# Two attention layers on one Trainium2 core: the first differential pair weighs its values one step of the lanes later

## What is computed

```python
z = rmsnorm(h) @ w_in[l]
c_q, c_kv, k_rope, dq, dk, dv, p_in, z_gate = split(z)
# latent attention (MLA), 8 heads of 64 + 32
q = (rmsnorm(c_q) @ w_uq);  kv = rmsnorm(c_kv) @ w_ukv
p = softmax(causal(scale * (q_nope k_nope + rope(q_rope) rope(k_rope))))
y_mla = p @ v
# differential attention, 8 heads with two maps each
p = softmax(causal(scale * dq dk - slope * distance))      # maps 0 and 1
y_diff = rmsnorm((p[0] - lam * p[1]) @ dv) * (1 - lambda_init)
y_pool = pool_mixer(p_in)
branches = [y_mla, y_diff, y_pool] @ w_branch;  gates = sigmoid(z_gate)
h = h + sum(gates * branches) @ w_out
```

## Time and profile before

| | |
|---|---|
| median of 3 runs | 2029.14 us (2028.71 to 2029.24) |
| the profiled execution | 2028.63 us, of which the span from first to last instruction is 2026.8 us |
| PE busy | 2015.5 us, 99% of the span |
| PEld, DVE, ACT busy | 84%, 69%, 50% |
| DMA engines busy | 54% by the hardware queue |
| granted clock of TensorE | 0.999 of full speed |
| mixer of layer 0 with its first visits, 236 to 380 us | PE 142.2, DVE 116.8, ACT 99.5 us of 144 |

### The profile page before, as it was taken

The page is one execution under the profiler, slowest core; times in us unless marked ns, Lnnn a source line. Parts: engine busy times, 40 slices in busy tenths (PEclk is TensorE's granted clock), DMA queues, the critical chain, the costliest instruction groups (busy, mean ns, idle before and its releaser), DMA issues.

```text
span 2026.8 us, 24812 instructions
## 1 busy us (share of the span) xinstructions
PE 2015.5 (99%) x10220; PEld 1701.7 (84%) x10220; DVE 1391.4 (69%) x1657; ACT 1022.1 (50%) x1218; POOL 88.5 (4%) x128
## 2 busy tenths in 40 slices
PE   9999999999999999999999999999999999999998
PEld 7888878888888888878888888888888888888887
DVE  6655697775757676787675667657767577577675
ACT  6444568453445345667453356654534466545331
POOL 1001010000010001100100000000100000000000
PEclk9999999999999999999999999999999999999999
DMA  9655544465656555444566574654655555555552
GB/s 335 212 187 169 174 164 146 162 207 195 193 182 224 192 179 192 159 147 162 195 209 197 167 230 136 207 167 170 243 196 188 189 174 187 167 186 202 193 187 83
DMA packets 225568, 377.64 MB, mean 186 GB/s; under 512 B 6624, under 2 KB 113248, under 8 KB 225456
## 3 DMA queue, kind: packets, MB, share of 16 engines
q1 hardware_dynamic: 221472, 362.64, 54.3%
q0 software_dynamic: 3984, 13.43, 2.0%
HBM read 374.99 MB, written 1.05 MB: 186 GB/s over the span
## 4 chain that ended last, share of the span: by engine, by line
PE 99%; DVE 1%; issue 0%; ACT 0%; DVEq 0%; POOL 0%; POOLq 0%
PE pb L1661 65%; PE pb L1678 18%; PE pb L1675 9%; PE pb L1687 2%; PE pb L1733 1%; PE pb L1812 1%; PE pb L1799 0%; PE pb L1811 0%; DVE wl L2119 0%; PE pb L1791 0%; PE pb L1650 0%; PE pb L1654 0%; PE pb L1692 0%; PE pb L1652 0%; PE pb L1819 0%
## 5 line engine op out<-in xcount | busy, mean ns | idle before, releaser
L1889 ACT ACTIVATE wh<-raw 128x2048 fp32r<-128x2048 f32 (+2 forms) x347 | 653.8, 1884 | 620.7 <-PE pb L1661 289.5
L2119 DVE TENSOR_TENSOR wl<-raw,wh 128x2048 fp32r<-128x2048 f32 (+2 forms) x345 | 774.7, 2253 | 149.0 <-ACT wh L1889 148.5
L1661 PE MATMUL pb<-wh,x 128*128 128x512 f32 (+1 forms) x2144 | 651.3, 386 | 0.0
L1661 PEld LDWEIGHTS pb<-wh,x 128*128 128x128 f32 x2144 | 400.8, 188 | 77.8
L1661 PE MATMUL pb<-wl,x 128*128 128x512 f32 (+1 forms) x1072 | 421.0, 393 | 0.0
L1678 PE MATMUL pb<-x,wh 128*128 128x512 f32 x1568 | 381.2, 392 | 0.0
L1678 PEld LDWEIGHTS pb<-x,wh 128*128 128x128 f32 x1568 | 287.6, 188 | 55.2
L1661 PE MATMUL pb<-wl,mh 128*128 128x512 f32 (+1 forms) x740 | 255.6, 391 | 0.0
L1661 PE MATMUL pb<-wh,ml 128*128 128x512 f32 (+1 forms) x740 | 253.7, 388 | 0.0
L1661 PE MATMUL pb<-wh,mh 128*128 128x512 f32 (+1 forms) x740 | 253.6, 388 | 0.0
L1661 PEld LDWEIGHTS pb<-wl,x 128*128 128x128 f32 x1072 | 201.5, 188 | 41.8 <-issue 3.7
(11 more groups left out here) (359 smaller groups left out, 1550.3 us busy)
## 6 DMA issues: line engine op xcount, KB each, us to landing
raw<-in_w_in_dram SPq DMA_DIRECT2D x100, 1024.0 KB, 5.2
raw<-in_w_ff_dram SPq DMA_DIRECT2D x64, 1024.0 KB, 5.4
raw<-in_ffn_w_down_dram SPq DMA_DIRECT2D x44, 1024.0 KB, 5.0
raw<-in_ffn_w_up_dram SPq DMA_DIRECT2D x42, 1024.0 KB, 5.3
raw<-in_ffn_w_gate_dram SPq DMA_DIRECT2D x41, 1024.0 KB, 5.3
raw<-in_w_branch_dram SPq DMA_DIRECT2D x24, 1024.0 KB, 5.0
raw<-in_w_out_dram SPq DMA_DIRECT2D x16, 1024.0 KB, 5.1
raw<-in_w_in_dram SPq DMA_DIRECT2D x4, 832.0 KB, 4.5
```

Source lines behind the costliest of these rows:

```text
L1661: ins = e.matmul(pb[b][:, 0:c1 - c0], x[:, s, cols], w[:, n, c0:c1], start=(it["first"] and n == 0 and q == 0), stop=(it["stop"] and n == ...
L1889: e.activation(hi, raw, ACT.Copy).then_inc(m.high_done, 1)
L2119: e.tensor_tensor(lo, raw, hi.bitcast(F32), ALU.subtract).then_inc(m.low_done, 1)
```

## The change

A `yield` more stands ahead of the weighing of the first pair of each layer. The generator returns there once, so the weighing, and with it all that lane 0 does later in this layer (the pairs 1 to 3 and, through it, `diff_end`), is added to the list one `pump()` later. No instruction is new and none is dropped; in both layers of the first block the same rows move. In what follows the lines of the changed kernel are two higher than those before from line 1013 on.

```diff
--- before.py
+++ after.py
@@ -1010,6 +1010,8 @@
             self.add("pcopy", dst=("lS", i, 1), use=uses[i], p=v["p"])
             yield
         while not self.pin_free or len(self.dv) < 2:
+            yield
+        if f == 0:
             yield
         w = self.side()
         v = self.pe("weigh2", kind="diff", lane=0, f=f, use=w, need=[("evac", uses[0]), ("evac", uses[1])] + self.dv)
```

## The result

The changed kernel takes 2036.26 us (median of 6 runs, 2035.90 to 2037.43) against 2029.01 us for the one before (6 runs, 2028.71 to 2030.22). The ratio is 1.0037, 95% interval 1.0025 to 1.0048: slower by 0.37%. The prediction said slower, 2034.1; the time lies 0.26 us above its range, and the move is half as large again as the one forecast. So the sign and, as will be seen, the two waits were right, and something that costs about 2 us was missing.

The account below looks back on a forecast made before the run. TensorE, busy 2015.5 of 2026.8 us, was taken as the bound. Closing its gap but meeting `lQ` waits gave 0.28 + 2.24 = 2.52 a layer, twice +5.0, on 2029.14: 2034.1 us; forecast's own range 2033.2 to 2035.6, overall 2029.5 to 2036.0.

Parts of the forecast that it names:

- The gap goes: First differential pair's weighing, each layer: TensorE runs on into `kvv`, -1.76 us; about 0.25 comes back at `kvk`'s bank.
- The maps wait behind the split: VectorE, second differential pair: its maps stand behind split `wl4_70` and start at 268.05, against 266.66 before.
- First latent scores: First latent pair: TensorE arrives at 276.2, waits 1.75 us for `lQ`, starts at 278.0; layer then stands at +0.28.
- No wait at the second and third pair: Second and third latent pairs: TensorE does not wait, as ScalarE had finished `lQ` well ahead; no added time.
- The stretch with `dsquare`: Third to fourth latent pair's scores: 2.38 us of `dsquare` moves in; 22.83 us against 20.59, TensorE waits 2.24 more.
- The sum: Whole kernel: 0.28 + 2.24 = 2.52 us a layer, in both layers, +5.0 us.
- The change leaves its work alone: TensorE, whole kernel: its work was taken as unchanged, since the edit adds and removes no instruction; no term for it.
- The view I named for it: Changed kernel's profile: L1811 waits of about 1.7 and 2.2 us per layer; granted clock below full tenths would refute.
- Rival D: TensorE's `dmean` behind `dsquare`: it also waits for the second half, another 1.19 us a layer, 2036.5; chance 0.10.
- B: First latent pair's wait comes back, the fourth's does not, ScalarE having idle time for `dsquare`: 2029.7 us; chance 0.14.
- C: Fourth latent pair's wait comes back, the first's does not: +0.7 or +1.6 us a layer, 2030.6 to 2032.4; chance 0.20.
- Rival A: The weighing's gap goes in both layers and nothing comes back: -1.76 us twice, 2025.6; chance 0.06.

Follow-up runs that it names:

- the last kernel: Against the kernel before: only the first weighing moved, behind `latent_kv` and ahead of the gates' first visit, later pairs and `dsquare` left in place; 2026.23 us, ratio 0.9983.
- the fill: Kernel before, with fourteen unused matmuls of 256 columns in the 1.76 us gap ahead of the first pair's weighing; 2029.07 us, ratio 0.9998.

## Where the prediction held and where it failed

- **The gap goes:** held. 1.76 and 1.78 at L1799 are gone, `kvk` pays 0.17 for the estimated 0.25.
- **The maps wait behind the split:** held to 0.1. VectorE, beside the earlier trace rows:

```profile
266.24 2.39 DVE L2121 TENSOR_TENSOR wl<-raw,wh 128x2048 fp32r<-128x2048 f32 x1 [1.87 <-ACT wh L1891]
268.67 0.56 DVE L2310 SCALAR_TENSOR_TENSOR lS<-dist,pb 128x384 f32<-128x384 f32 x1
```

  268.67 - 0.52 = 268.15 for 268.05 in the prediction (whose terms, 265.70 and 2.30, add up to 268.00).
- **First latent scores:** the wait was put at 1.75 and is 1.31; the start, 278.36 - 0.52 = 277.84, for 278.0. TensorE gained less ahead of it than I thought, and got there at 276.53 for 276.2, for its matmuls took 0.32 longer on the way; and `lQ` ended 0.16 earlier. As `lQ` sets the start, the first of these cost nothing.
- **No wait at the second and third pair:** held, but the third's scores stand at 330.40 - 0.52 = 329.88, 0.52 later than the earlier trace rows, for 0.28. There is no wait in these 0.24. They are TensorE's own: from the first latent scores to the third its matmuls take 0.48 longer than before, against which stand the 0.16 of the earlier `lQ` and a turn that costs 0.25 for the 0.33 assumed.
- **The stretch with `dsquare`:** the term that carried the sum held to the hundredth. ScalarE, beside the earlier trace rows:

```profile
277.94 0.37 ACT L2024 ACTIVATE lQ<-pb 96x256 f32<-96x256 f32 x1
...
335.01 0.62 ACT L1991 ACTIVATE sq<-yd 128x512 f32<-128x512 f32 x1
...
337.38 0.58 ACT L2038 ACTIVATE G<-pb 128x512 f32<-128x512 f32 x1
...
352.87 0.37 ACT L2024 ACTIVATE lQ<-pb 96x256 f32<-96x256 f32 x1
```

  From the scores at 330.40 to the end of `lQ` at 353.24 it took 22.84 us (22.83 predicted), and the scores follow 22.89 after the scores, 20.64 before: 2.25 more for 2.24. That TensorE came later, and so waited 1.95, did not matter, for `lQ` sets this start as well.
- **The sum:** 2.78 in layer 1 and 4.41 - 1.57 = 2.84 in layer 0 for 2.52, so 5.6 for 5.0 without the clock. Most of the 0.6 are the 0.24 above, counted twice (0.48).
- **What failed is the step from a wait to its price.** The sum 0.28 + 2.24, twice, has no term for the clock. I priced a wait of TensorE at its own length, and let the clock appear only in the last sentence, as something that would make the prediction wrong, with neither a price nor a chance. The runs show a wait of 1.95 us to cost up to 3.5: its length, and 1.57 for a stretch of about 3.4 us at 1.2 GHz behind it. With one such fall in each run, as the time of the six runs suggests and the one trace shows, 5.0 + 0.6 + 1.6 = 7.2, against 7.25 measured.
- **A second step failed by less.** "The change leaves its work alone" is true of the matmuls and not of their time: 1.1 us a layer more, of which 0.6 vanish in the two waits and 0.5 stay.
- **The view I named for it could not have shown it.** The row PEclk of the page reads 9 in all forty slices after, too: a slice is 51 us, and the fall lasts 3.4. It shows in windows of a microsecond and in the matmuls' own durations, and less surely in the mean granted clock to three digits.
- **Rival D** gave 2036.5, near the truth, but for a wait at `dmean` that the list of waits does not have. It is not what happened. **Rivals B and C** fall with both waits present. **Rival A**, the gap gone and nothing coming back, is what the last kernel does: 2.9 us for 3.5. So the rule named with it (the Trainium skill, "Perfetto Trace Analysis", section "Optimization Strategy": find the gaps of the engine that binds and what blocks it) leads here to the right gap; what the gap is worth depended on what else the edit moved.
- **Evidence I had:** the three times of the kernel before, 2028.71 to 2029.24, all lay in its lower group. Only more runs showed that its gap of 1.76 us has a like price, 1.45 us, in 18 of the 58 that came with the experiments.

## To carry to other kernels

In this kernel the gap on the engine that binds was worth closing only where what moved with it kept its distance from the next hand-over without slack; that was a wait of 0.26 us in the weight loads' timeline, and the move put 2.4 us of another engine's work into the stretch ahead of it. When work is put off in a hand-made order, list every item that follows it in its lane and each engine's queue at the place where it lands; then look whether the one item can be moved alone, which is what the last kernel does. And a wait on TensorE is priced with a fall of the clock behind it as a case of its own, with a chance from the spread of the runs. Work that is only moved can take longer, too: 1.1 us a layer here, found by setting each matmul beside its counterpart.

## What the runs showed of the chip

- The granted clock fell to 1.2 GHz for about 3.4 us behind waits that TensorE spent idle, in some executions and not in others. Three falls stand in traces, behind waits of 1.95, 1.97 and 2.48 us; behind the gap of 1.76 us of the kernel before they are inferred from the times and from the fill. By the times falls came in 9 of 25 and 9 of 33 runs of the kernel before, in all 6 of the changed one, in 6 of 10 with the change in layer 1 alone, in 4 of 10 with the split held, in at least 4 of 7 with the yield dropped, in none of 10 where the longest wait was 1.3 us. Each cost 1.3 to 2.1 us; why the price differs is not shown. In the three traces the fall came 1.5 to 1.8 us after the engine had resumed, not at once.
- Matmuls without use in the wait kept the clock up in all 17 runs that had them; in the traced fill of the changed kernel the scores started within 0.12 us of the same place.
- The same matmuls took longer, by up to 0.2 us each, where small groups stood beside other neighbours: in all 1.11 to 1.20 us a layer with the pairs late, 0.22 and 0.24 with the one weighing moved.
- Two profiled executions can differ by 0.5 us from the first weights on, as the clock rises at a slightly different moment at the start (matmuls of 0.79 us at 4.84 after, 0.67 at 4.77 before).
